# Unit-matrix products in TensorE's queue ahead of waits and inside the first attention, the rotary stage of the second layer shifted, and the last weighting one step earlier

## The reference

```python
def hybrid_layer(x, ...):                       # first block, once
    proj = rmsnorm(x) @ w_in
    y_a = dilated_attention(...)                # 6 heads of 64, causal, bias by distance
    y_b = gla(...)                              # gated linear attention, a scan
    y_c = moba_attention(...)                   # 6 heads of 64; for 512 tokens causal as well
    x = x + concat(y_a, y_b, y_c) @ w_out
    return x + square(relu(rmsnorm(x) @ w_ff1)) @ w_ff2

def attend(q, k, v):                            # second block, 8 heads on 2 key heads
    s = einsum('bkgqd,bksd->bkgqs', q, k) * HEAD_DIM ** -0.5
    return einsum('bkgqs,bksd->bkgqd', softmax(s), v)

for l in range(2):                              # second block
    ux, uc = (rmsnorm(x) * (1 + sc_a) + sh_a) @ w_in, (the same for ctx)
    mix = concat(fourier_mix(ux), attention(rotary(q), rotary(k), v), hgrn_scan(ux))
    x = x + g_a * (mix @ w_out)
    x = x + g_f * swiglu(rmsnorm(x) * (1 + sc_f) + sh_f)
```

## Time and profile before

| what | value |
|---|---|
| median of 3 runs (lowest, highest) | 2574.51 us (2569.66, 2586.59) |
| the profiled execution's own time | 2582.34 us |
| its span | 2580.6 us |
| mean granted TensorE clock | 0.939 of full |
| busy PE / PEld / DVE / ACT / POOL | 2409.3 / 1839.2 / 1035.7 / 777.5 / 802.8 us |
| PE idle at L739 for DVE's a_lo L661, in all | 25.3 us in 13 waits, longest 4.2 |

### The profile page before, as it was taken

One profiled execution on the slowest core, in us unless ns is written; L12 is line 12 of the kernel. 1 busy time (PEld: TensorE's weight loads), 2 busy tenths in 40 slices (PEclk: granted clock), 3 DMA queues, 4 the chain that ended last, 5 costly groups with the idle time before them and its releaser, 6 DMA issues.

```text
span 2580.6 us, 35232 instructions
## 1 busy us (share of the span) xinstructions
PE 2409.3 (93%) x15254; PEld 1839.2 (71%) x15254; DVE 1035.7 (40%) x1475; ACT 777.5 (30%) x953; POOL 802.8 (31%) x279
## 2 busy tenths in 40 slices
PE   7987899999999999889899999999799989899998
PEld 5763367777887883458788888888487446688886
DVE  7654446255255426622523323312452743311113
ACT  4322233123234314423311121112433533322222
POOL 3322243333442214302222222222222413343432
PEclk9985699999999998889999999999899879999999
DMA  6530034443222101012023322311211003222221
GB/s 217 187 123 18 17 138 156 163 163 116 98 73 92 42 1 48 2 51 74 33 98 115 115 98 83 146 54 37 92 41 48 2 2 114 82 98 98 98 90 57
DMA packets 36411, 218.11 MB, mean 85 GB/s; under 512 B 4152, under 2 KB 7016, under 8 KB 13088
## 3 DMA queue, kind: packets, MB, share of 16 engines
q1 hardware_dynamic: 32968, 209.44, 22.5%
q10 hardware_dynamic: 3288, 6.41, 0.7%
HBM read 213.70 MB, written 2.14 MB: 84 GB/s over the span
## 4 chain that ended last, share of the span: by engine, by line
PE 77%; DVE 6%; ACT 3%; issue 1%; POOL 1%; DMA 0%; DVEq 0%; ACTq 0%; POOLq 0%
PE PS L739 61%; PE PS L1228 2%; PE PS L1255 2%; PE PS L754 2%; DVE s_states L1635 1%; DVE a_lo L661 1%; DVE tmp L668 1%; PE PS L1940 1%; PE PS L1832 1%; PE PS L1272 1%; PE PS L2053 1%; PE PS L1240 1%; PE PS L849 1%; ACT w_hi L917 1%; DVE x L681 1%
## 5 line engine op out<-in xcount | busy, mean ns | idle before, releaser
L2189 POOL TENSOR_TENSOR w_lo<-raw,w_hi 128x2048 fp32r<-128x2048 f32 (+3 forms) x163 | 666.0, 4091 | 1464.0 <-ACT w_hi L917 1464.0
L739 PE MATMUL PS<-a_hi,w_hi 128*128 128x512 f32 (+1 forms) x2104 | 695.0, 372 | 45.3 <-DVE a_lo L661 25.3
L739 PE MATMUL PS<-a_lo,w_hi 128*128 128x512 f32 (+1 forms) x2104 | 685.3, 367 | 0.0
L739 PE MATMUL PS<-a_hi,w_lo 128*128 128x512 f32 (+1 forms) x2104 | 683.3, 366 | 0.0
L739 PEld LDWEIGHTS PS<-a_hi,w_hi 128*128 128x128 f32 x2104 | 367.6, 191 | 130.4 <-issue 54.5
L739 PEld LDWEIGHTS PS<-a_hi,w_lo 128*128 128x128 f32 x2104 | 365.1, 191 | 66.7
L739 PEld LDWEIGHTS PS<-a_lo,w_hi 128*128 128x128 f32 x2104 | 364.4, 191 | 63.3 <-issue 1.7
L917 ACT ACTIVATE w_hi<-raw 128x2048 fp32r<-128x2048 f32 (+1 forms) x145 | 270.3, 1864 | 324.3 <-PE PS L739 114.6
L739 PE MATMUL PS<-hid_hi,w_hi 128*128 128x512 f32 (+1 forms) x784 | 259.3, 367 | 1.6 <-issue 1.6
L739 PE MATMUL PS<-hid_hi,w_lo 128*128 128x512 f32 (+1 forms) x784 | 258.9, 366 | 0.0
L739 PE MATMUL PS<-hid_lo,w_hi 128*128 128x512 f32 (+1 forms) x784 | 258.4, 366 | 0.0
(11 more groups left out here) (228 smaller groups left out, 2339.7 us busy)
## 6 DMA issues: line engine op xcount, KB each, us to landing
raw<-in_w_ada SPq DMA_DIRECT2D x48, 1024.0 KB, 6.8
raw<-in_w_ff SPq DMA_DIRECT2D x32, 1024.0 KB, 4.9
raw<-in_w_in SPq DMA_DIRECT2D x22, 1024.0 KB, 4.9
raw<-in_w_gate SPq DMA_DIRECT2D x22, 1024.0 KB, 4.9
raw<-in_w_up SPq DMA_DIRECT2D x22, 1024.0 KB, 5.0
raw<-in_w_down SPq DMA_DIRECT2D x16, 1024.0 KB, 4.8
raw<-in_w_out SPq DMA_DIRECT2D x12, 1024.0 KB, 5.0
raw<-in_w_down SPq DMA_DIRECT2D x8, 768.0 KB, 4.2
```

The costliest lines, as they stand in the source:

```text
L739: mm = p.matmul(ps[:, dst], wv[:, k, idx * P:(idx + 1) * P], av[:, k, dst], start=first, stop=last)
L2189: pool.tensor_tensor(low[:, ks, :], whole[:, ks, :], high[:, ks, :].bitcast(F32), ALU.subtract).then_inc(tell.sem, 1)
```

## The change

It adds products of the unit matrix `ident` with itself (128 x 128 by 128 columns, fp32) at eight places of `gemm_pe`, behind `slot_free` and ahead of the waits for k: 14 in `in1`, 28 in `ff1_0`, 30 in `ff2_0_0`, `in2_1` and `ff2_1_0`, 22 in `out1`, `out2_0` and `out2_1`; and 40 at the head of the first attention. They write to a PSUM area that the next real product overwrites. It adds six products of a zero corner of `ident` (64 x 64 by 128 columns, fp32) ahead of `turned(s)`, added to the open values, in 17 ticks of the first attention and in ticks 2 and 3 of each of the other two. It delays `early_pe` and `early_act` of layer 1 by ten ticks, moves a small DVE instruction behind `early_dve`, and lets DVE weight the last group of the second and third attention one tick earlier.

```diff
+        FILL_BEHIND = {"in1": 14, "out1": 22, "ff1_0": 28, "ff2_0_0": 30, "in2_1": 30, "out2_0": 22, "out2_1": 22, "ff2_1_0": 30}
+
+        def keep_busy(p, ps, n):
+            for _ in range(n):
+                p.matmul(ps[:, 0:P], ident[:], ident[:], start=True, stop=True)
...
                 if rising is not None and name.startswith("out"):
                     for n in job_of[i]:
                         slot_free(n)
+                    keep_busy(p, slot(job_of[i][0]), FILL_BEHIND[name])
                     for k in range(kt):
                         p.wait_ge(rising.sem, rising.at(k + 1))
...
                     for n in job_of[i]:
                         slot_free(n)
+                    keep_busy(p, slot(job_of[i][0]), FILL_BEHIND.get(name, 0))
                     for turn, side in enumerate(sides):
...
+            def add_zeros(s, n):
+                if s >= 2 and steps[s - 1][0] == steps[s - 2][0]:
+                    g = steps[s - 1][0]
+                    for _ in range(n):
+                        p.matmul(values_ps(plan, g)[groups[g]["heads"][0]["rows"], 0:P], ident[0:HD, HD:P], ident[0:HD, :],
+                                 start=False, stop=False)
+
+            if causal:
+                keep_busy(p, scores_ps(plan, 0), 40)
             for u in plan["units_at"][0]:
                 scores(u)
...
                 if s < len(steps):
+                    if causal or s < 4:
+                        add_zeros(s, 6)
                     turned(s)
...
-                late = 1 if causal else 3
-                if s >= late and s - late < len(steps) and steps[s - late][3]:
+                late = 1 if causal else 2 if s > len(steps) else 3
+                if s >= late and s - late < len(steps) and steps[s - late][3] and not (s - late == len(steps) - 1 and late == 3):
...
+        FIRST_TICK = (0, 10)
...
         def early_pe(p, l):
             S = lambda n: local(("early", l), n)
+            for _ in range(FIRST_TICK[l]):
+                yield
...
         def early_act(a, l):
             S = lambda n: local(("early", l), n)
+            for _ in range(FIRST_TICK[l]):
+                yield
...
-                if l == 1:
-                    plus_one(1, 32)
                 if l == 0:
...
                 run(early_dve(v, l))
+                if l == 1:
+                    plus_one(1, 32)
```

## The result

| | before | after |
|---|---|---|
| median of the runs | 2574.5 us (3) | 2642.5 us (3; 2641.5 to 2643.7) |
| ratio, 95% interval | | 1.0266 (1.0239 to 1.0293) |
| profiled execution, its span | 2582.3, 2580.6 | 2642.5, 2640.7 |
| mean granted clock | 0.939 | 0.938 |

A forecast was written before the change was run, and what follows sets the result against it. PE was taken as the bound, with 77% of the chain that ended last. The terms -3.7 + 2 + 0 + 7.7 + 4 - 10 - 1.3 = -1.3 us, applied to the median, gave 2573 us; range 2552 to 2610.

The forecast's parts named there:

- f = 0.8: First attention: with the zero products, share f of the stage at 2.4 GHz becomes 0.8, from 0.24; -3.7 us.
- 40 products: Head of the first attention: they end at 181.1, scores needed at 179.42; +2 us (0 to 3.5).
- rival A: First attention: the zeros do not lift the clock; +34 us in the stage, 2611 in all; chance 0.28.
- The formula: First attention: cost less gain of the zeros by share f at full clock, about 50.5 - 68 f us.
- the price of a product at half clock: One unit-matrix or zero product, 128 columns in two records, was priced at 0.44 us at half clock.
- the share on the path: First attention: 0.87 of the zero products' time lengthens the path, 38.6 us at half clock, 21.3 at full.
- Rotary: Layer 1, rotary stage ten ticks later: DVE's roundings run through, PE starts panel three earlier; -10 us (8 to 12 gained).
- Second and third attention with the weighting: Zeros in ticks 2 and 3: +4 us for both attentions (1 to 8); weighting one tick earlier: -1.3 (0 to -4.5).
- Out fills: 22 products each at out1, out2_0, out2_1, behind the waits for weights: +4, +1.7 and +2, sum +7.7 us (6 to 13).
- Norm fills: Fills at the five norms: a late start is caught up while DVE feeds the first panel; 0 us.
- Rival B: First attention: PE at full clock throughout, changes of group too; stage gives 17 us back, 2560 in all; chance 0.27.
- Rival C: Delayed rotary work is caught up at the end of in2_1 and its 10 us come back; 2583; chance 0.05.

The follow-up runs named there:

- e2: Changed kernel with each zero product on all 128 rows of the unit matrix in place of 64: 2598.0 us, 1.0101 against before.
- e10: Changed kernel with twelve zero products on 64 rows in place of six in each such tick of the first attention: 2672.9 us, 1.0382 against before.
- e1: Changed kernel without any of the zero products, all else kept: 2598.4 us, 1.0108 against before.
- e3: Kernel before with only layer 1's rotary stage ten ticks later and the small DVE instruction moved behind it: 2575.7 us, ratio 1.0007.
- e12: Kernel before with POOL's w_lo cut to 16 of each 256 columns in five in2_1 panels, plus the rotary shift: 2562.2 us, ratio 0.9943.
- e11: Kernel before with POOL's w_lo cut to 16 of each 256 columns in five in2_1 panels, no rotary shift: 2573.7 us, ratio 0.9995.
- e6: Kernel before with only the 22 products ahead of each of out1, out2_0 and out2_1: 2596.1 us, ratio 1.0104.
- e15: Kernel before, unchanged, run once more for a second profile: 2567.9 us.
- e5: Kernel before with only the fills behind the five norms (14, 28, 30, 30, 30 products): 2577.6 us, ratio 1.0018.
- e13: Kernel before with the rotary shift and POOL's w_lo made in four instructions in five in2_1 panels, whole computation kept: 2569.9 us, ratio 0.9987.

## Why the prediction was wrong

**The step that failed is the choice f = 0.8**: "I take it that the extra work keeps the clock through most of a group". The rows for the other side were already in the prediction: a PE busy 4.00 of 4.00 us at 0.50. I took them as a reason to doubt and not to decide. Such a short row can't decide alone (in e2 PE is busy 4.00 of 4.00 us at 0.50 from 252 to 256 and has full clock at 260); the 20 of 20 us of e10 do. And what I set against it was misread: the fast steps in the earlier trace rows, from 301.61 on, are the fifth group's, and behind its change the sixth begins at half clock again (2.13 us at 317.69, as at 212.79). So no group had kept the clock across a change by itself. The stage measured +34.4 with the 40 products, and f, from a mean clock of 0.59 to 0.62, stayed at 0.2. That is rival A, with its price of 34 (e1: the zeros' own part is 32). What A had as its second reason, that the corner uses a quarter of the array, e2 bears out on the side of the rows, as far as rows and contents can be parted; whether the 64 output columns matter too no run shows. The formula held at that end: the price of a product at half clock (0.44, measured 0.46) and the share on the path (0.87; 32 of the 40.2 us are 0.80). At f = 0.54 (e2's 0.77) it gives +14 for the stage and with the 40 products +16; measured +6.7, so there it was too dear by some 9. The products of e2 stood where the clock was high more often than f says, 31.1 us for all 102 where the formula has 33; that is 2 of the 9, and the rest is open.

The Trainium skill, "TensorE: Matmul & The Clock Gate", section "What's actually happening", ties the gate to how busy PE has been. Here the rows disagree if any product counts as busy: e10 has PE busy 90% of the stage at 0.60, e2 83% at 0.77.

**Even with A the sum was some 23 us short** of the profile's 60, and 31 of the 68 by the medians. Step by step:

- Rotary: -10 forecast, -0.6 (e3: -0.2). Failed at "Then DVE's roundings run through, 5.6 sooner". I put the 5.57 us down to ACT, which the bracket names, and didn't look at what DVE's own instruction did behind it: it took 1.18 us in place of 0.48 and ended 0.28 behind POOL's w_lo, which ran from 1832.71 to 1837.27. With POOL out of the way the term measures 9.9 (e12 against e11).
- Second and third attention with the weighting: +4 - 1.3 forecast, +8.7 and +7.0 measured. The zeros were mis-sized: 12 products at 0.46 are 5.5 in each layer, all at half clock, and nothing of it fell in waits. The weighting's mechanism was right (the wait goes to L1826), its sign not: the products behind the longer wait were slower, +1.5 and +0.9 in the mean. These two make 13.4 of the 15.7. They don't prove that split: e1, without the zeros, has +10.2 in the second attention, and e10, with all of both, has +1.5 in the third, as wide as the scatter above.
- Out fills: +7.7 forecast, 5.5 + 1.3 + 4.5 = 11.3, with the 1.0 from the end of out1 12.3. Mechanism right, size low at out2_1, which I had called 2: there too the fill waited for w_lo first. By the medians e6 cost 21.7, and the half of it that lies outside the sites has no cause shown.
- 40 products: +2, measured 1.4, at the edge of the scatter. Norm fills: 0, measured 0.1 at ff1_0, caught up as forecast (the -1.9 ahead of 165 is no effect, e15 has -2.0 there); e5 in all +3.2, not told from none.
- The step from profile to median was off as well: both profiles taken as they are give 60, the medians 68, since the profiled execution of before lay 8 above its median, and the stated range was put around the median.

Rival B (full clock throughout) is out: no run's mean clock in this stage passed 0.8. Rival C, the rotary gain given back, is what happened, but not in the way named: not for a lack of ticks, but in DVE's way past POOL.

## What to carry to other kernels

Before filling PE's waits to keep its clock, look in the trace for a long stretch that is fully busy and still slow: it says that such work doesn't lift the clock there, and more of it is pure cost. Where the trace has only a short one, add the filler in one stage alone and read the granted clock first. A fill belongs ahead of the wait that ends last, and is no longer than it. Where a bracket names one releaser, look also at the duration of the waiting engine's own instruction: one far over its usual length is a second wait, and taking away one of two that end together gives nothing.

## What the runs showed of the hardware

**DVE waits for a POOL instruction that is under way.** It shows on DVE instructions with two inputs from SBUF; the rounding of the hidden rows shows it in the kernel before:

```profile
414.77 4.82 POOL L2189 TENSOR_TENSOR w_lo<-raw,w_hi 128x2048 fp32r<-128x2048 f32 x1 [15.43 <-ACT w_hi L917]
415.96 4.18 DVE L1045 TENSOR_TENSOR hid_lo<-tmp,hid_hi 128x512 fp32r<-128x512 f32 x1 [0.83 <-ACT hid_hi L977]
422.42 0.69 DVE L1045 TENSOR_TENSOR hid_lo<-tmp,hid_hi 128x512 fp32r<-128x512 f32 x1 [0.83 <-ACT hid_hi L977]
```

4.18 us under POOL's instruction, 0.69 without. All seven of L1045 with 512 columns that began well inside a w_lo instruction took 4.18 to 4.24 us and ended 0.55 behind it; the 256 columns of L661 above ended 0.28 behind. DVE instructions with one input from PSUM were not longer there (nine of L1042: 0.69, as elsewhere; nine of L1028: 0.75, as elsewhere). The Trainium skill, "SBUF — State Buffer", section "Who interferes with whom", says the same: a DVE instruction with two SBUF inputs contends with a GpSimd instruction that reads SBUF. The trace agrees, and with POOL's work in four pieces (e13) DVE's instructions took 1.0 to 1.8 us.

**Rows and the clock.** Six zero products a tick on 64 rows: 0.59; twelve: 0.60; none: 0.59 (the kernel before has 0.61 and 0.57 in its two profiles, 181 to 336 us); six on 128 rows: 0.77; three on 128 rows: 0.64.

**Scatter.** One program's profiles differed by 14.5 us of span (and its runs by some 20), with the granted clock of one stage at 0.79 and 0.84. In the attentions of the second block a term under 7 us can't be read from a pair of profiles, while in in2_1 one of 2 us can: what a pair can show has to be found for each stage.
